# Head 0 of the attention stage: another order of its steps, earlier loads, and the prefix sums of the cached forget logits by TensorE

## The reference, cut to what matters

```python
h = rmsnorm(x, norm_mix)
q, k, v, f_logit, xr, gr = split(h @ w_in)           # 8 heads of 64
logf = log_sigmoid(f_logit + b_forget)
# attention with a logit bias: s = q k^T / 8 + c_q - c_k,  c = cumsum(logf)
# prompt: causal over 2064 tokens.  sample: one query over 4096 cached keys and its own
c = cumsum(concat([logf_past, logf]))                 # logf_past = cache_logf[page_table]
rnn = rg_lru_branch(xr, gr)                           # conv, gates, linear recurrence
x = x + concat(rmsnorm(att), rmsnorm(rnn)) @ w_out
x = x + (gelu(conv(g)) * val) @ w_ffn_down            # g, val = rmsnorm(x) @ w_ffn_up
```

## Time and profile before

| | us |
|---|---|
| median of 3 runs | 3130.68 (3129.87 to 3131.41) |
| the profiled execution | 3136.74 |
| its span | 3135.0 |

### The profile page before, as it was taken

How to read it: one execution, slowest core, us unless ns; L and a number is a source line. 1 busy time by engine, 2 the same in 40 slices (tenths; PEclk the granted TensorE clock), 3 DMA queues, 4 the chain that set the end, 5 groups by cost and what they waited for, 6 DMA issues and landing times.

```text
span 3135.0 us, 44458 instructions
## 1 busy us (share of the span) xinstructions
PE 2950.3 (94%) x15701; PEld 2590.0 (83%) x15701; DVE 1378.8 (44%) x1896; ACT 757.0 (24%) x1525; POOL 1222.9 (39%) x589
## 2 busy tenths in 40 slices
PE   4999999877899999979999999999999999999998
PEld 4899999744455555559999999999999998999998
DVE  5312444476667776233165445444544552222221
ACT  7000333322233333341020000000000004443442
POOL 1111011167777777037662222222222214444443
PEclk9999999978899999989999999999999999999999
DMA  7222333347788888544441111111111115555553
GB/s 225 75 73 82 113 115 109 105 139 231 231 271 271 268 259 259 163 157 128 139 146 43 46 47 49 46 40 54 47 46 42 54 51 197 191 187 173 187 197 106
DMA packets 247894, 420.37 MB, mean 134 GB/s; under 512 B 44573, under 2 KB 152298, under 8 KB 243234
## 3 DMA queue, kind: packets, MB, share of 16 engines
q1 hardware_dynamic: 166850, 320.50, 32.3%
q10 hardware_dynamic: 80616, 97.07, 9.2%
q0 software_dynamic: 288, 1.05, 0.1%
HBM read 335.13 MB, written 83.46 MB: 134 GB/s over the span
## 4 chain that ended last, share of the span: by engine, by line
PE 76%; POOL 6%; DVE 6%; SPq 4%; issue 3%; DMA 3%; ACT 3%; ACTq 0%; POOLq 0%; DVEq 0%
PE PS L2565 35%; PE PS L2230 15%; PE PS L2653 5%; PE PS L2655 4%; PE PS L2654 4%; PE PS L2449 3%; POOL prod L943 3%; SPq L605 2%; DVE MP L1848 1%; PE PS L2556 1%; SPq L598 1%; DVE YT L2179 1%; DVE scw L1858 1%; PE PS L2433 1%; PE PS L2473 1%
## 5 line engine op out<-in xcount | busy, mean ns | idle before, releaser
L2565 PE MATMUL PS<-MH,VS 128*128 128x416 f32 (+1 forms) x4000 | 1080.4, 351 | 3.1 <-issue 3.1
L2565 PEld LDWEIGHTS PS<-MH,VS 128*128 128x128 f32 x4000 | 749.4, 188 | 13.3 <-issue 4.7
L2565 PE MATMUL PS<-ML,VS 128*128 128x416 f32 (+1 forms) x2000 | 699.6, 350 | 0.0
L2565 PEld LDWEIGHTS PS<-ML,VS 128*128 128x128 f32 x2000 | 376.0, 188 | 2.6 <-issue 0.8
L1096 POOL TENSOR_TENSOR DL<-DR,DH 128x1408 fp32r<-128x1408 f32 x80 | 258.6, 3233 | 287.4 <-ACT DH L1519 287.3
L943 POOL TENSOR_TENSOR prod<-Kpg,qb 128x1024 f32<-128x1024 f32 x128 | 303.2, 2369 | 84.2 <-DMA Kpg<-in_cache_k 31.8
L1025 POOL CAST VS<-VR 128x1024 fp32r<-128x1024 f32 x52 | 62.9, 1209 | 689.1 <-PE PS L2565 687.5
L2653 PE MATMUL PS<-GH,DH 128*128 128x416 f32 (+1 forms) x880 | 315.5, 358 | 15.0 <-DVE GL L2161 7.6
L2449 PE MATMUL PS<-PT,VA 128*65 128x416 f32 (+16 forms) x816 | 319.0, 474 | 4.0 <-ACT PT L1382 3.4
L2655 PE MATMUL PS<-GH,DL 128*128 128x416 f32 (+1 forms) x880 | 311.3, 354 | 0.0
L2654 PE MATMUL PS<-GL,DH 128*128 128x416 f32 (+1 forms) x880 | 309.8, 352 | 0.0
(11 more groups left out here) (286 smaller groups left out, 4288.2 us busy)
## 6 DMA issues: line engine op xcount, KB each, us to landing
Kpg<-in_cache_k SPq DMA_DIRECT2D x256, 256.0 KB, 4.4
Vpg<-in_cache_v SPq DMA_DIRECT2D x256, 256.0 KB, 4.8
DR<-in_w_down SPq DMA_DIRECT2D x80, 704.0 KB, 4.1
gT<-GO ACTq DMA_DIRECT2D x110, 208.0 KB, 2.0
VR<-in_w_up SPq DMA_DIRECT2D x44, 512.0 KB, 3.5
GRb<-gT SPq DMA_DIRECT2D x31, 416.0 KB, 5.1
WR<-in_w_stream SPq DMA_DIRECT2D x21, 512.0 KB, 3.5
GRa<-gT SPq DMA_DIRECT2D x24, 416.0 KB, 5.6
```

The lines of the kernel that those rows point to most:

```text
L2565: mm = e.matmul(PS[:, j, 0:full(j)], w[:, u, k], x[:, k, j * BW:j * BW + full(j)], start=(k == 0 and q == 0), stop=(k == KC - 1 and q == 2))
```

## The change

1. **Loads.** The keys of head 0 go into `K0`, a view of `AO`, which is moved in memory to lie over weight slot 1, free once chunk 19 is done: they and the page numbers load before chunk 20 ends. The decay rows are put together in `Kst2` instead of `rden`, whose memset waits only for the recurrence's last product (`r_y`). SP, not ScalarE, issues the last `mixT<-RX`. The first key pages load at the last projection matmul, in two parts, before `phase_end` 4; GpSimd makes products 0 and 1 before `phase_end` 4.
2. **Prefix sums.** A constant `prior` (ones strictly above the diagonal inside each block of 32) gives, in one matmul per half, the sum over earlier pages; it is transposed (`earlier_rows`) and added by a ones matmul into the same PSUM bank as the triangle's. VectorE's `segm`, scan, subtraction and adds fall away; it adds only the new token's bias (`new_bias`). The steps come at pieces 24, 28, 31, 33, 38, 42 (`CACHED`); ScalarE evicts eight banks per half instead of six.
3. **Order.** Eight instead of four scores of sample 0 come among the pieces (`EARLY`), the other eight at tiles 3 to 13, its softmax at tiles 15 to 22, its page steps from tile 24; sample 1's first four scores at 18 to 22, the rest from 28 to 45. GpSimd makes sample 1's products 0 to 3 before the head mask and before the second part of `prepare(1)`; `load_order` puts its keys earlier.

```diff
-EARLY = (32, 36, 40, 43)
+EARLY = (14, 18, 22, 26, 32, 36, 40, 43)
+CACHED = (24, 28, 31, 33, 38, 42)
@@ attention_plan
-    plan[28 if first else 4].append(("weight sum", 0))
+    plan[22 if first else 4].append(("weight sum", 0))
-                plan[g + 1].append(("scores", g))
-            plan[25 + (22 * g) // 15].append(("scores", 16 + g))
+                plan[3 + 3 * (g - len(EARLY)) // 2].append(("scores", g))
+            plan[18 + 3 * g // 2 if g < 4 else 28 + 17 * (g - 4) // 11].append(("scores", 16 + g))
-                plan[27 + 23 * g // 15].append(("pages", g // 2))
+                plan[23 + 27 * g // 15].append(("pages", g // 2))
-        for t, step in ((21, "end"), (22, "turn"), (23, "top"), (24, "spread max"), (25, "less"), (26, "exps"), (27, "sums")):
+        for t, step in ((15, "end"), (16, "turn"), (17, "top"), (18, "spread max"), (19, "less"), (20, "exps"), (21, "sums")):
@@ load_order
-            at = 26 + 1.5 * (n - 4)
+            at = 17 + 1.6 * (n - 4)
@@ sync
+            e.wait_ge(g_mm, 5 * (NIN - 1))
+            e.dma_start(K0[0:HD], kT[0:HD, :]).then_inc(st_ld, 16)
+            e.dma_start(K0[HD:P], kT[0:HD, :]).then_inc(st_ld, 16)
+            e.dma_start(pgid[:], a["page_table"]).then_inc(pg_ld, 16)
+            e.dma_start(pgcol[:], a["page_column"]).then_inc(pg_ld, 16)
             e.wait_ge(r_sc, 4)
 ...
             e.wait_ge(r_y, 5)
-            e.dma_start(Kst2[0:HD], kT[0:HD, :]).then_inc(st_ld, 16)
-            e.dma_start(Kst2[HD:P], kT[0:HD, :]).then_inc(st_ld, 16)
+            e.dma_start(mixT[DM - P:DM, :], RX[:, 3:3 + TP]).then_inc(r_st, 16)
             e.wait_ge(c_att2, 1)
-            e.dma_start(rden[HD + 2:HD + 4], decayT[:, 0, :]).then_inc(x_first, 16)
+            e.dma_start(Kst2[HD + 2:HD + 4], decayT[:, 0, :]).then_inc(x_first, 16)
 ...
-            for g in range(4):
+            e.wait_ge(g_mm, 5 * NIN)
+            for g in range(2):
                 fetch_first_keys(g)
+            e.wait_ge(t_ev, 49)
+            e.wait_ge(t_pe, 53)
+            fetch_query(0, 0)
+            for g in range(2, 4):
+                fetch_first_keys(g)
+            e.wait_ge(phase_end, 4)
@@ gpsimd
-            e.wait_ge(r_st, 65)
-            e.memset(rden[HD:HD + 4], 1.0).then_inc(c_att2, 1)
+            e.wait_ge(r_y, 5)
+            e.memset(Kst2[HD:HD + 4], 1.0).then_inc(c_att2, 1)
 ...
+            e.wait_ge(r_st, 65)
+            e.memset(rden[HD:HD + 4], 1.0).then_inc(c_att2, 1)
 ...
+            pool_products(0, 0, 0, 2)
             e.wait_ge(phase_end, 4)
 ...
-            pool_products(0, 0, 0, 4)
+            pool_products(0, 0, 2, 4)
 ...
             pool_products(0, 0, 8, 16)
+            pool_products(1, 1, 0, 4)
 ...
-            e.wait_ge(cb_ok, 1)
             prepare(1, 1, 3, 7)
-            pool_products(1, 1, 0, 16)
+            pool_products(1, 1, 4, 16)
@@ vector
+            def new_bias(g):
+                if g == 0:
+                    e.wait_ge(lf_ld, 16)
+                e.wait_ge(lf_tp, 8 * g + 8)
+                own = slice(4 * g, 4 * g + 4)
+                e.tensor_tensor(cb[0:1, own, 0, :], cnew[0:1, own], PS[0:1, 6, 0:4 * NH].rearrange("p (h s) -> p s h", s=4),
+                                ALU.add).then_inc(cb_ok, 1)
-            g_steps.inc(e.memset(segm, 1.0))
-            g_steps.inc(e.tensor_tensor_scan(incl, segm, ctot, 0.0, ALU.mult, ALU.add))
-            g_steps.inc(e.tensor_tensor(incl, incl, ctot, ALU.subtract))
-            for h in range(NH):
-                ins = e.tensor_tensor(cwith[:, h], incl.rearrange("p (h s g) -> p h s g", h=NH, g=PAGES)[:, h], cwith[:, h],
-                                      ALU.add)
@@ tensor
+                for b in range(2):
+                    e.matmul(PS[:, 4 + b, :], prior[:], lpage[:, g, 512 * b:512 * b + 512], start=True, stop=True)\
+                        .then_inc(lf_tp, 1)
+            def earlier_rows(g):
+                by_head = earlier.rearrange("p (s h) -> p h s", h=NH)
+                for b in range(2):
+                    for h in range(4):
+                        mm = e.transpose(PS[:, 6 + b, h * P:(h + 1) * P], by_head[:, 4 * b + h], identF[:])
+                    mm.then_inc(lf_tp, 1)
             def cached_sums(g):
+                for x in (xtp, earlT):
+                    e.matmul(PS[:, 6, 0:4 * NH], onesF[:], x[:, PAGES - 1:8 * P:PAGES], start=x is xtp, stop=x is earlT)
                 for b in range(2):
-                    e.matmul(PS[:, 4 + 2 * b, :], triu[:], xtp[:, 512 * b:512 * b + 512], start=True, stop=True)
-                    e.matmul(PS[:, 5 + 2 * b, :], onesF[:], xtp[:, 512 * b:512 * b + 512], start=True, stop=True)\
-                        .then_inc(lf_tp, 1)
+                    part = slice(512 * b, 512 * b + 512)
+                    e.matmul(PS[:, 4 + b, :], triu[:], xtp[:, part], start=True, stop=False)
+                    e.matmul(PS[:, 4 + b, :], onesF[:], earlT[:, part], start=False, stop=True).then_inc(lf_tp, 1)
```

149 lines of the change are left out of this document (77 added, 72 removed).

## The result

The changed kernel takes 3103.64 us in the median of 4 runs (3100.16 to 3108.8), the kernel before 3130.57 in the same job: a ratio of 0.9914 with a 95% interval of 0.9900 to 0.9928. That is 26.9 us less, where 22 were forecast (3109, range 3094 to 3126). The profiled execution of the changed kernel took 3101.6 us, with a span of 3099.9.

A forecast was written before the change was run, and what follows sets the result against it. One stretch of about 200 us binds, GpSimd's products to VectorE's reductions, with transfers first late, then crowded. The parts put head 1 at 788 instead of 810.06, 22 us less: 3130.7 to 3109, range 3094 to 3126.

The forecast's parts named there:

- part 5: Rest of head 0: sample 1's 12 products at the old pace end at 774.8, head 1 starts at 788, not 810.06.
- Part 1: Start of attention: keys' load and decay rows leave the chain; first piece at 620.8 instead of 626.96, 6.2 us earlier.
- rival D: Start not brought forward: ScalarE's stores wait behind earlier key pages, 4 to 6 us lost, 3114; no separate chance given.
- Part 2: Stretch of the maxima: 53.5 us plus 2.4 (reductions) and about 8.8 (sums on TensorE), 64.7 us; first tile at 685.5.
- rival B: Maxima eat the gain: whole stretch at 1.2 GHz, first tile at 701 to 703, 5.5 us less, 3125; chance 0.12.
- Part 3: After the last piece: VectorE's scan, subtraction and adds go; tile 5 at 691.5 instead of 694.22.
- GpSimd's side effect: GpSimd's copy beside VectorE's scan took 5.83 us, later 1.91; 3.9 us of GpSimd's time come back, off the path.
- Part 4: GpSimd's chain in head 0: `prepare(1)` ends at 730.3 instead of 738.0, first page step at 732.5 instead of 749.37.
- rival C: Slower: SP's loads queue behind `prepare(1)`, ending at 746, then bytes take 72 us; 8 us more, 3139; chance 0.07.
- The named risk: Head 0's page steps: the prediction would be wrong if value pages held TensorE for long; no size given.
- The claim that heads 1 to 7 keep their length: Behind head 0: heads 1 to 7 stay at 78 us each; the prediction would be wrong if they changed.
- Rival A: Head 0 as tight as a later head: head 1 starts at 771, 39 us less, 3092; chance 0.14.

The follow-up runs named there:

- e1: Changed kernel, but GpSimd's memset of the decay rows waits again for the recurrent branch's last store to land: 3114.0 us.
- e2: Changed kernel with the first two of sample 0's value blocks that wait for a page step loaded earlier, ahead of the next head's load: 3115.09 us.
- e5: Changed kernel with the matmuls with `prior` cut to 32 of 512 columns and one transpose instead of four per bank (decay wrong): 3104.89 us.
- e6: Changed kernel with four instead of eight of sample 0's reductions among the pieces, the other twelve at tiles 3 to 14: 3109.58 us.
- e7: Changed kernel with VectorE work like the removed scan, subtraction and adds put back on scratch data: 3111.53 us.
- e10: Changed kernel with sample 2's products 0 to 3, made by GpSimd at the end of head 0, each made three times: 3117.28 us.
- e11: Changed kernel with each matmul with `prior` made three times and each transpose of `earlier_rows` twice: 3106.25 us.
- e8: Changed kernel with the second part of `prepare(1)` before sample 1's first products and head 2's load ahead of sample 1's keys 4 and on: 3100.04 us.
- e9: Changed kernel with `prepare(1)`'s second part and head 2's load earlier as in e8, and the head mask after sample 1's last product: 3102.54 us.
- e3: Changed kernel with the order of before (`EARLY`, head 0's steps, load order, GpSimd's order), keeping the new start and sums: 3123.65 us.

## Why the prediction was right, and where it wasn't

**The bound** was read rightly. The time was lost on one stretch of 200 us, by GpSimd's chain first and crowded transfers then, and every kernel above that delays `prepare(1)` pays for it. The seven edited kernels that leave GpSimd's order up to `prepare(1)` as it is (e1, e2, e5, e6, e7, e10, e11) and the changed kernel's two profiles reach head 1 55.3 to 59.8 us after `prepare(1)` ends, whether it ends at 726 or at 735; in the nine the DMA engines are busy for 0.89 to 0.93 of that time. That alone can't tell the transfers from GpSimd's 12 products, since sample 1's last product ends 38.5 to 41.4 us behind `prepare(1)` in all nine; what tells them apart is which engine waits at the end (part 5). And it holds only while `prepare(1)` ends at 726 or later: in e8 and e9 it ends some 19 us earlier, and head 1 comes 1.0 to 1.5 us earlier.

**Part 1, the start: right.** Forecast 620.8, measured 619.95, and what comes last is the row named:

```profile
617.92 1.94 ACT L1317 ACTIVATE KA<-AO 64x2080 fp32r<-64x2080 f32 x1 [0.71 <-ACT TS L1246]
```

It begins 0.96 us earlier than in the earlier trace rows, so ScalarE's waits for its stores did not grow, and rival D did not come. But the carrier of the gain was not TensorE's piece, which is all that the step followed: e1 loses 2.0 us there and more behind it, by GpSimd.

**Part 2, the maxima: the term that was mis-sized.** Forecast 64.7 us, measured 54.75 and 58.46, against 53.63 before. The 2.4 us for four reductions can't be seen in e6 and e3. The 8.8 us for the sums are about what they took on TensorE (`prior` 3.25 + 1.98, the transposes 1.05 + 1.05, the narrow ones 1.48, so 8.8 in all; the narrow ones have 32 columns of 512, a sixteenth and not an eighth, and still took 0.77 and 0.71 us a half where 0.3 to 0.5 stood), yet TensorE's busy time in the stretch rose only from 41.39 to 44.01 us. So all the rest of its work took some 6.2 us less, at a clock of 0.75 instead of 0.66. In the second profile, at 0.71, the busy time is 47.27 us and the rest took 2.9 less: the size of this saving is not firm. The step priced the added work at both clocks and left the old work at the price of before. The Trainium skill's rule weighed there ("TensorE: Matmul & The Clock Gate", section "What's actually happening", activity lifts the clock) goes with this as far as the rows show: the clock stood at 0.50 until some 640 us, was 0.69 in the 7 us from 640 with `prior` in them, and 1.00 from 647 to 668. What I made of it, the low price for the whole stretch (11.2 us, rival B), did not come. These are the slices:

```profile
633.00:640.00 7.00, 5.45 (x12) 2.88 (x13) 6.11 (x10) 0.00 (x0) 5.53 (x3) 0.50 0.94 343
640.00:647.00 7.00, 6.18 (x19) 3.80 (x18) 3.40 (x7) 2.39 (x4) 6.65 (x3) 0.69 0.03 10
647.00:654.00 7.00, 6.72 (x29) 3.94 (x28) 3.25 (x7) 2.61 (x4) 6.62 (x3) 1.00 0.13 31
```

**Part 3, the tail of the sums: right, and worth more than it said.** Head 1's first piece is at 682.18 without a wait, 9.3 us before the forecast 691.5: tile 0 came 10.8 us early, 10 of them from part 2, and the piece lay 7.5 us behind it instead of 6. The first three parts together were to give only 2.7 us, since part 2 took back what they gained; put back, the block costs 7.9 us (e7). GpSimd's side effect was called off the path, and this was wrong: a product of 6.15 us and a wait of 7.88 us for the reduction behind the block delay `prepare(1)` by 8.4 us. Without the block the copy of the earlier trace rows takes 1.91 us:

```profile
668.54 1.91 POOL L941 CAST QA<-Qst 64x2080 fp32r<-64x2080 f32 x1 [0.17 <-POOL KA L939]
```

This agrees with the section "Key points" of the Trainium skill's "GPSIMD Engine Reference", which the prediction had drawn on: 6.15 and 5.83 beside the scan, 2.36 and 1.91 without.

**Part 4, GpSimd's chain: right, 1 to 4 us pessimistic.** `prepare(1)` ended at 726.12 and 729.20 against 730.3. Products 8 to 15 ran from 670.66 to 692.65 without a wait for keys or reductions, so that one started after 690 where four had been forecast. That tile 0 came 10 us too early for the sum hardly reached `prepare(1)`: in e11 it is 6.9 us later and `prepare(1)` 2.9. That the mis-sized part 2 did not spoil the total is in part luck. The first page step came at 720.11 against 732.5, and this turned out to be worth nothing: in the kernel with the cut sums it came at 731.88 and head 1 at 783.36, 0.6 us later than with 720.11. There the value pages that TensorE waits for, 16.5 us in the changed kernel, are waited for 7.3 us.

**Part 5, the rest of head 0: the right answer by a sum whose parts were off.** Sample 1's last product ended at 765.3, forecast 774.8, and head 1 came 17.4 us behind it, not 12.7, at 782.73 against 788. The sum had taken the products for what ends last, as they did in the kernel before, where TensorE waited 7.15 us for sample 1's maxima. Now it is the reverse: VectorE has the maxima of sample 1 at 772.61 + 0.63 and then waits 6.44 us for TensorE,

```profile
772.61 0.63 DVE L1924 TENSOR_REDUCE mloc<-scw 128x8 f32<-128x264 f32 x1
779.68 0.28 DVE L1929 TENSOR_REDUCE mtop<-PS 8x1 f32<-8x128 f32 x1 [6.44 <-PE PS L2451]
```

and TensorE has only been held up by value pages, the last time here; from the end of `prepare(1)` to head 1 it is busy for 40.0 of 56.6 us and waits for them for 16.5:

```profile
774.28 1.93 PE L2508 MATMUL PS<-Vpg,scw 128*32 128x512 f32 x8 [3.13 <-DMA Vpg<-in_cache_v]
```

So rival C came nearer to the mechanism (SP's queue behind `prepare(1)`, bytes and not products), with a wrong size: 57 us and not 72. That the bytes and not TensorE's own work set the 57 is argued from these waits, not shown: in e5 TensorE waits only 7.3 us for value pages and is busy for 49.8 of 57.3 us, and head 1 is no earlier. The sum came near 788 by parts that were off both ways: `prepare(1)` was 4.2 us and the rest up to the last product 5.3 us too late, the step from there to head 1 4.7 us too short. The 72 us of before were a DMA share of 0.84 at 259 GB/s, the 56.6 after are 0.93 at 292: 18.7 MB against 16.5, so fewer bytes are left at that point and they go faster.

**The named risk** that value pages would hold TensorE for long came true, 16.5 us with one of 9.75; e2, which moves the wait without shortening it, gains nothing and loses 11.5 us, so what the wait costs was not measured. **The claim that heads 1 to 7 keep their length** was wrong, by 13.7 and 8.7 us in the two profiles, 7.3 and 3.9 of it in head 1, where the clock is the cause that the rows show. For the others no cause was looked for. The gain is more than the spread between profiles: from head 1 to stage 3 it is 559.6 to 567.4 us in the eleven profiles that have the new order and nothing added behind it (all but e3 and e10), 573.3 in the kernel before and 571.7 in e3, which has the order of before. So some 6 to 14 us go with the new order of head 0, and no part of the sum had them. Both points are ones of which the prediction had said that it would be wrong if they came: its total held, and its account of what comes last and of what stands behind head 0 did not.

**Rival A** (3092, head 0 as tight as a later one) did not come: its head 1 would start at 771. The rows have what stood against it, a DMA share of 0.93 from `prepare(1)` to head 1.
